# Order of the modulation and first products, and 32-column levels of the RWKV inverse, in a two-layer diffusion block

## The chip, the core and the metric

The kernel runs on one NeuronCore of a Trainium2 chip. The engines are TensorE (PE, its weight loads are listed as PEld), VectorE (DVE), ScalarE (ACT), GpSimd (POOL) and SyncE (SP, which only issues transfers here). The metric is the device time of one execution in microseconds (us), as the median of several runs. All arrays are 32-bit floats; PE multiplies either in full fp32 or, for the large weight products, as three fp32r products of high and low parts.

## What is computed

A hybrid block of two layers over 256 context and 256 latent tokens of width 1024. The parts that matter here:

```
mod_l = jnp.split((jax.nn.silu(c) @ ada_w[l] + ada_b[l])[:, None, :], 6, axis=-1)
mod_c = jnp.split(jax.nn.silu(c_ctx) @ ada_w[l] + ada_b[l], 6, axis=-1)
hl = modulate(rmsnorm(xl, norm_mix_pre[l]), mod_l[0], mod_l[1])     # h * (1 + scale) + shift
hc = modulate(rmsnorm(xc, norm_mix_pre[l]), mod_c[0], mod_c[1])
zl = hl @ w_in[l]
zc = hc @ w_in[l]
...
def step(s, inp):                       # branch D, RWKV-7, both directions
    r_t, w_t, k_t, v_t, kk_t, a_t = inp
    sa = jnp.einsum('bhvk,bhk->bhv', s, kk_t)
    s = (s * w_t[:, :, None, :] - sa[..., None] * (kk_t * a_t)[:, :, None, :]
         + v_t[..., None] * k_t[:, :, None, :])
    return s, (jnp.einsum('bhvk,bhk->bhv', s, r_t) if emit else None)
```

The kernel runs the recurrence in chunks of 64 tokens. Each chunk needs the inverse of a unit lower triangular 64x64 matrix, one for each of 4 heads and 8 chunks.

## The kernel before

**The first stage.** Everything is stored with features on the 128 partitions and the 512 tokens along the free axis, so the normalised input has 8 row tiles (k = 0 to 7) of 128x512. The shift and scale of row tiles 2q and 2q+1 come from two 256-column blocks of `ada_w`, blocks q and 4+q: this is modulation pair q. A pair is made on PE by two `mod` jobs (L1921, 8 products each) and two `modt` jobs (L1929, 2 products each) that fold four partial rows and turn them to columns. Between them ACT copies the row out of PSUM (`mrow`, L912), and after them DVE adds the bias (L1337) and forms the gain (`amod`, L1413). ACT then applies shift and scale to two row tiles (L953), rounds them to fp32r (`HR` high, L959), DVE makes the low part (L1401), ACT and DVE split two new tiles of `w_in` into `whi` (L899) and `wlo` (L1326). PE multiplies: `steps(ns, ks)` takes the output tiles ns over the row tiles ks, with three instructions for each pair (L1950, L1951, L1952). There are 6 output tiles in this stage (FIRST), so 6 x 8 x 3 = 144 products. Each engine works its list in order; ACT and DVE have the order pair q, its two row tiles, its two weight tiles, pair q+1. SP issues the loads in one queue: `ada` has 4 slots, so the blocks of pair 2 wait for the `mod` jobs of pair 0, those of pair 3 for the `mod` jobs of pair 1; behind them stand the constants and the next weight tiles. A weight slot of `ring` is free when its two `wlo` are made.

After the stage the remaining output tiles of z follow in `project` (L1878 to L1880), then attention, RWKV, gates, output projection and FFN, for two layers.

**The inverse.** For each layer and direction (4 passes) the inverse TN of all blocks starts at block size 2 and doubles over LEVELS = (2, 4, 8, 16, 32). A level z is, for each head pair p of two:

- `sx` (PE, L2120): LM1, stationary, times TN, moving, in 16 small products of 64x64, four of them side by side in the array
- a mask into XS (DVE, L1652) that keeps the block under the diagonal at this level
- `tt` (PE, L2108): four transposes of TN, copied to TT by ACT (L1153)
- one or several other jobs that are laid between (LM2 products L2082, `tok` transposes, `ta`, `xv`, `wl`/`al`, `kss`)
- `sy` (PE, L2159): TT, stationary, times XS, moving, again 16 products of 64x64
- TN = TN - sy (DVE, L1669)

PE takes sx p0, sx p1, tt p0, tt p1, the other jobs, sy p0, sy p1. DVE takes the two masks, other work, the two subtractions. sx of the next level waits for the subtraction of its p. After the last level two more transposes, and from them u0 and at, lead to the chain over the 8 chunks. XS has 64 columns for each block; only the columns whose block of size z is an even one (t // z even) can be other than zero after the mask.

Of the kernel before, what the change touches and what calls it, by code (L numbers as in the profile page):

```python
# [17 lines left out]
ALU = mybir.AluOpType  # L18
# [3 lines left out]
P = 128  # L22
# [4 lines left out]
LAT = 256  # L27
# [8 lines left out]
CH = 64  # L36
NCH = T // CH
NB = T // P
# [31 lines left out]
for _n, _c in VEC_COLS:  # L70
# [4 lines left out]

CONST_COLS = [("ones", P), ("fold", 2), ("ident", P), ("heads", P), ("swap", P), ("lm", 2 * CH), ("m1", CH),
              ("m2", CH), ("m4", CH), ("m8", CH), ("m16", CH), ("m32", CH), ("eye", CH), ("cos", LAT), ("sin", LAT),
# [21 lines left out]
def constants():  # L99
# [3 lines left out]
    def put(name, a):  # L103
        c[:, CON[name]:CON[name] + a.shape[1]] = a
# [13 lines left out]
    for z in LEVELS:  # L118
        put(f"m{z}", ((s // z) % 2 == 1) & (t // z == s // z - 1))
# [229 lines left out]
def build(nc, a, out):  # L349
    ctx = ExitStack()  # L350
    with ctx:
# [108 lines left out]
        XS = at("XS", 88, [2, 2, NB, CH])  # L460
# [124 lines left out]
        def bank(name):  # L585
            k = PLACE[name]
            return ps[:, k:k + 2, :] if name[0] in PAIRED else ps[:, k, :]

# [274 lines left out]
        def _(act):  # L863
# [96 lines left out]

            for q in range(4):
                fill(("start", 0, q))
                first_rows(2 * q)
                first_rows(2 * q + 1)
                first_high(2 * q)
                first_high(2 * q + 1)
                if q < 3:
                    split_until(2 * q + 2)
            for l in range(LAYERS):
# [339 lines left out]
        def _(dve):  # L1309
# [110 lines left out]
            for l in range(LAYERS):  # L1420
# [200 lines left out]
                for d in range(2):  # L1621
# [12 lines left out]

                    def square_mask(name):
                        return K(name, CH).unsqueeze(1).unsqueeze(1).to_broadcast([P, 2, NB, CH])
# [12 lines left out]
                    for n, z in enumerate(LEVELS):  # L1649
                        for p in range(2):  # L1650
                            s = blocks(filled(dve, ("sx", l, d, z, p)))
                            dve.tensor_tensor(XS[:, p, :, :, :], s, square_mask(f"m{z}"), ALU.mult)\  # L1652
                               .then_inc(frees(("sx", l, d, z, p)), 1)
# [8 lines left out]
                        for p in range(2):  # L1662
                            s = blocks(filled(dve, ("sy", l, d, z, p)))
                            t = TN[:, p, :, :, :].rearrange("p b y n -> p y b n")
                            if n:
                                emptied(dve, ("sy", l, d, LEVELS[n - 1], p))
                            else:
                                dve.wait_ge(t_done, 2 * it + p + 1)
                            dve.tensor_tensor(t, t, s, ALU.subtract).then_inc(frees(("sy", l, d, z, p)), 1)  # L1669
# [161 lines left out]
        def _(pe):  # L1831
# [101 lines left out]
            def first_products():  # L1933
# [22 lines left out]
                fill(("start", 0, 0))  # L1956
                steps(range(2), range(2))
                fill(("start", 0, 1))
                steps(range(2), range(2, 4))
                steps(range(2, 4), range(4))  # L1960
                fill(("start", 0, 2))
                steps(range(4), range(4, 6))
                steps(range(4, 6), range(6))
                fill(("start", 0, 3))
                steps(range(FIRST), range(6, KT))

            pe.wait_ge(silu_c, 1)
            for l in range(LAYERS):
# [96 lines left out]
                for d in range(2):  # L2065
# [45 lines left out]
                    for n, z in enumerate(LEVELS):  # L2111
                        for p in range(2):
# [6 lines left out]
                            for b, x, y in corners():  # L2119
                                last = pe.matmul(o[side(y), x, CH * b:CH * b + CH], LM1[side(x), 2 * p + y, b, 0:CH],  # L2120
                                                 TN[side(x), p, b, y, :], start=True, stop=True)
# [32 lines left out]
                        for p in range(2):  # L2154
# [3 lines left out]
                            for b, x, y in corners():  # L2158
                                last = pe.matmul(o[side(x), y, CH * b:CH * b + CH], TT[side(y), p, b, x, :],  # L2159
                                                 XS[side(y), p, x, b, :], start=True, stop=True)  # L2160
# [177 lines left out]
```

## Time and profile before

| | |
|---|---|
| runs, median (lowest to highest) | 1743.99 us (1742.7 to 1755.26), 3 runs |
| the profiled execution's own time | 1740.77 us, span 1739.0 us |
| mean granted TensorE clock | 0.973 |
| busy share of the span | PE 93%, PEld 76%, DVE 53%, ACT 45%, POOL 17% |

The span runs from the first to the last instruction. The profile page divides it into 40 slices, follows the chain that ended last, and groups instructions by line. Since PE is busy nearly everywhere, the stretches to look at are those in which it is not: the first 100 us, and the four passes of the inverse at about 350, 420, 1285 and 1348 us.

### The profile page before, as it was taken

The page shows a single profiled execution, that of the slowest core. Times are in us where ns is not written, and L with a number is a line of the kernel's source. Part 1 is how long each engine was busy: PE and PEld are TensorE (multiplying, and loading weights), DVE is VectorE, ACT ScalarE, POOL GpSimd, SP SyncE. Part 2 cuts the span into 40 slices and gives each one's busy share as a digit, 9 for nine tenths or more (in the row PEclk, how much of TensorE's full clock was granted, in tenths as well). Part 3 has the DMA queues.
Part 4 walks back from the last instruction along what each step waited for, and adds up shares of the span by engine and source line. Part 5 has one row for each costly group of instructions (what it writes and reads, how often), then busy time and mean ns, then how long its engine had stood idle before and what let it go on. Part 6 is the DMA issues. An engine that isn't in the chain of part 4 may idle for free.

```text
span 1739.0 us, 33048 instructions
## 1 busy us (share of the span) xinstructions
PE 1611.8 (93%) x14136; PEld 1321.1 (76%) x14136; DVE 913.3 (53%) x1438; ACT 783.1 (45%) x1285; POOL 302.3 (17%) x241
## 2 busy tenths in 40 slices
PE   5899999988899998899999998999988889989997
PEld 3678767776666676688888885887776679879997
DVE  3154445476334444555555224565786446567754
ACT  4232355473342233544444223624766453566653
POOL 0041033513010000011112000121452110012201
PEclk8899999999899999999999999999999999989999
DMA  9473345504682222132222534734523284436553
GB/s 324 107 190 98 112 159 176 176 7 148 185 301 73 96 73 73 49 97 97 97 97 62 124 100 148 222 124 134 168 66 124 55 278 155 145 98 194 182 164 116
DMA packets 230496, 234.49 MB, mean 135 GB/s; under 512 B 5904, under 2 KB 217232, under 8 KB 230224
## 3 DMA queue, kind: packets, MB, share of 16 engines
q1 hardware_dynamic: 210720, 190.17, 34.6%
q0 software_dynamic: 15024, 35.92, 7.6%
q10 hardware_dynamic: 4608, 6.29, 1.1%
q8 instruction: 113, 1.85, 0.5%
q14 instruction: 31, 0.25, 0.0%
HBM read 216.63 MB, written 15.73 MB: 134 GB/s over the span
## 4 chain that ended last, share of the span: by engine, by line
PE 67%; DVE 5%; issue 3%; ACT 3%; DMA 0%; POOL 0%; ACTq 0%; DVEq 0%; POOLq 0%
PE ps L1878 16%; PE ps L1879 16%; PE ps L1880 16%; PE ps L2262 5%; PE ps L2120 2%; PE ps L2108 1%; PE ps L1921 1%; PE ps L2159 1%; DVE X L1392 1%; PE ps L2082 1%; PE ps L1901 1%; DVE wlo L1326 1%; PE ps L1902 1%; PE ps L1903 1%; PE ps L1859 1%
## 5 line engine op out<-in xcount | busy, mean ns | idle before, releaser
L899 ACT ACTIVATE whi<-ring 128x1024 fp32r<-128x1024 f32 (+1 forms) x264 | 275.3, 1046 | 550.7 <-PE ps L1880 493.1
L1326 DVE TENSOR_TENSOR wlo<-ring,whi 128x1024 fp32r<-128x1024 f32 (+1 forms) x264 | 326.5, 1242 | 218.5 <-ACT whi L899 217.8
L1878 PE MATMUL ps<-H,whi 128*128 128x512 f32 (+1 forms) x656 | 220.6, 336 | 2.2 <-DVE wlo L1326 2.2
L1880 PE MATMUL ps<-H,wlo 128*128 128x512 f32 (+1 forms) x656 | 220.4, 336 | 0.0
L1879 PE MATMUL ps<-H,whi 128*128 128x512 f32 (+1 forms) x656 | 220.4, 336 | 0.0
L1878 PE MATMUL ps<-HR,whi 128*128 128x512 f32 (+1 forms) x568 | 202.2, 356 | 2.2 <-DVE wlo L1326 1.8
L1880 PE MATMUL ps<-HR,wlo 128*128 128x512 f32 (+1 forms) x568 | 198.3, 349 | 0.0
L1879 PE MATMUL ps<-HR,whi 128*128 128x512 f32 (+1 forms) x568 | 198.1, 349 | 0.0
L1878 PEld LDWEIGHTS ps<-H,whi 128*128 128x128 f32 x656 | 124.5, 190 | 15.6 <-issue 2.8
L1880 PEld LDWEIGHTS ps<-H,wlo 128*128 128x128 f32 x656 | 124.5, 190 | 12.9
L1879 PEld LDWEIGHTS ps<-H,whi 128*128 128x128 f32 x656 | 124.5, 190 | 12.5
L1878 PEld LDWEIGHTS ps<-HR,whi 128*128 128x128 f32 x568 | 107.5, 189 | 20.0 <-issue 5.4
L1879 PEld LDWEIGHTS ps<-HR,whi 128*128 128x128 f32 x568 | 107.6, 189 | 14.0 <-issue 0.7
L1880 PEld LDWEIGHTS ps<-HR,wlo 128*128 128x128 f32 x568 | 107.5, 189 | 14.1
L799 POOL TENSOR_SCALAR pr<-pr,stat 128x512 f32<-128x512 f32 (+1 forms) x48 | 71.3, 1498 | 246.4 <-DVE stat L1597 246.4
L1878 PE MATMUL ps<-UA,whi 128*128 128x512 f32 (+1 forms) x320 | 107.6, 336 | 0.0
L1879 PE MATMUL ps<-UA,whi 128*128 128x512 f32 (+1 forms) x320 | 107.5, 336 | 0.0
L1880 PE MATMUL ps<-UA,wlo 128*128 128x512 f32 (+1 forms) x320 | 107.5, 336 | 0.0
L855 POOL TENSOR_TENSOR CU<-CU,rs 128x512 f32<-128x512 f32 (+1 forms) x22 | 39.5, 1796 | 373.3 <-ACT rs L1294 373.3
L1878 PE MATMUL ps<-HG,whi 128*128 128x512 f32 (+1 forms) x256 | 91.7, 358 | 0.0
L2262 PE MATMUL ps<-YB,WB 128*128 128x512 f32 (+1 forms) x256 | 87.0, 492 | 4.2 <-DVE YB L1755 4.2
L1879 PE MATMUL ps<-HG,whi 128*128 128x512 f32 (+1 forms) x256 | 86.7, 339 | 0.0
(318 smaller groups left out, 3064.2 us busy)
## 6 DMA issues: line engine op xcount, KB each, us to landing
ring<-in_ffn_up SPq DMA_DIRECT2D x44, 1024.0 KB, 5.1
ring<-in_ada_w SPq DMA_DIRECT2D x40, 1024.0 KB, 5.6
ring<-in_w_gate SPq DMA_DIRECT2D x32, 1024.0 KB, 6.1
ring<-in_w_in SPq DMA_DIRECT2D x24, 1024.0 KB, 7.2
ring<-in_ffn_down SPq DMA_DIRECT2D x32, 512.0 KB, 4.0
ada<-in_ada_w SPq DMA_DIRECT2D x8, 1024.0 KB, 11.9
WB<-in_w_branch POOLq DMA_DIRECT2D x8, 1024.0 KB, 7.5
ring<-in_w_o SPq DMA_DIRECT2D x8, 1024.0 KB, 5.2
```

What stands on the lines that cost most here:

```text
L799: pool.tensor_scalar(pr[:, u % 4, 0:nk], pr[:, u % 4, 0:nk], stat[:, 2, u % 4:u % 4 + 1], None, ALU.mult).then_inc(p_ready, 1)
L855: pool.tensor_tensor(u, u, (rs, rt)[j % 2][:, c0:c1], ALU.mult).then_inc(u_ready, 1)
L899: act.activation(whi[half_slot(m)][:, 0:kn, :], ring[:, SLOT[raw] % RING, 0:kn, P * half:P * half + P], ACT.Copy).then_inc(hi_done, 1)
L1326: dve.tensor_tensor(wlo[half_slot(m)][:, 0:kn, :], ring[:, SLOT[raw] % RING, 0:kn, P * half:P * half + P], whi[half_slot(m)][:, 0:kn, :].b ...
L1392: ins = dve.scalar_tensor_tensor(x, O[:, i - 1, 256 * s:256 * s + 256], amod[:, k, i - 1, s:s + 1], x, ALU.mult, ALU.add)
L1859: last = pe.matmul(o[:, c0:c1], K("ones"), src[:, i, c0:c1], start=(i == 0), stop=(i == KT - 1))
L1878: pe.matmul(o[:, c0:c1], hi[:, i, :], part(0, k), start=(k == 0), stop=False)
L1879: pe.matmul(o[:, c0:c1], hi[:, i, :], part(1, k), start=False, stop=False)
L1880: last = pe.matmul(o[:, c0:c1], lo[:, i, :], part(0, k), start=False, stop=(k == kn - 1))
L1901: pe.matmul(o, hi[:, k, :], part(0, k)[:, c0:c1], start=(k == 0), stop=False)
L2120: last = pe.matmul(o[side(y), x, CH * b:CH * b + CH], LM1[side(x), 2 * p + y, b, 0:CH], TN[side(x), p, b, y, :], start=True, stop=True)
L2262: last = pe.matmul(o[:, c0:c1], wb[:, 2 * i + k, P * (j % 2):P * (j % 2) + P], YB[:, 2 * i + k, c0:c1], start=(k == 0), stop=(k == 1))
```

## The change

Two things are changed.

In the first stage, PE makes modulation pair 1 before any product, and pair q+1 before the products with the row tiles of pair q. `steps` is cut accordingly. ACT's code is written in another order, too, but its instructions come out in the same order as before, and so do those of DVE and SP.

In the inverse, sx multiplies only the even blocks of TN's columns (a strided moving operand), so it streams 32 columns and not 64; its mask constants, XS and the sy product have 32 columns for each block; and the subtraction touches only the even blocks of TN (again strided). The helper `even_blocks` picks these columns.

```
+CH2 = CH // 2
     for z in LEVELS:
-        put(f"m{z}", ((s // z) % 2 == 1) & (t // z == s // z - 1))
+        even = t[:, (t[0] // z) % 2 == 0]
+        put(f"m{z}", ((s // z) % 2 == 1) & (even // z == s // z - 1))
...
+        def even_blocks(v, z):
+
+            if len(v.shape) == 2:
+                return v.rearrange("p (g two n) -> p g two n", two=2, n=z)[:, :, 0, :]
+            return v.rearrange("p b y (g two n) -> p b y g two n", two=2, n=z)[:, :, :, :, 0, :]
...
-                            s = blocks(filled(dve, ("sx", l, d, z, p)))
-                            dve.tensor_tensor(XS[:, p, :, :, :], s, square_mask(f"m{z}"), ALU.mult)\
+                            s = filled(dve, ("sx", l, d, z, p))[:, :, 0:NB * CH2].rearrange("p x (b n) -> p x b n", b=NB)
+                            dve.tensor_tensor(XS[:, p, :, :, :], s, half_mask(f"m{z}"), ALU.mult)\
...
-                            s = blocks(filled(dve, ("sy", l, d, z, p)))
-                            t = TN[:, p, :, :, :].rearrange("p b y n -> p y b n")
+                            s = filled(dve, ("sy", l, d, z, p))[:, :, 0:NB * CH2]                                .rearrange("p y (b g n) -> p b y g n", b=NB, n=z)
+                            t = even_blocks(TN[:, p, :, :, :], z)
...
                 fill(("start", 0, 0))
+                fill(("start", 0, 1))
                 steps(range(2), range(2))
-                fill(("start", 0, 1))
-                steps(range(2), range(2, 4))
-                steps(range(2, 4), range(4))
+                steps(range(2, 4), range(2))
                 fill(("start", 0, 2))
-                steps(range(4), range(4, 6))
-                steps(range(4, 6), range(6))
+                steps(range(4), range(2, 4))
+                steps(range(4, 6), range(4))
                 fill(("start", 0, 3))
+                steps(range(FIRST), range(4, 6))
                 steps(range(FIRST), range(6, KT))
...
-                                last = pe.matmul(o[side(y), x, CH * b:CH * b + CH], LM1[side(x), 2 * p + y, b, 0:CH],
-                                                 TN[side(x), p, b, y, :], start=True, stop=True)
+                                last = pe.matmul(o[side(y), x, CH2 * b:CH2 * b + CH2].rearrange("k (g n) -> k g n", n=z),
+                                                 LM1[side(x), 2 * p + y, b, 0:CH], even_blocks(TN[side(x), p, b, y, :], z),
+                                                 start=True, stop=True)
```

On PE, at the start of the first stage, the list before is (`whi_70` to `whi_75` are the high parts of output tiles 0 to 5, `wlo_76` to `wlo_81` the low ones; line numbers of the changed kernel are 12 higher here):

```order
L1921 MATMUL ps<-ada,cpad 32x256 x16
L1929 MATMUL ps<-con,mrow 128x2 x4
L1950 MATMUL ps<-HR,whi_70 128x512
L1951 MATMUL ps<-HR,whi_70 128x512
L1952 MATMUL ps<-HR,wlo_76 128x512
...
L1950 MATMUL ps<-HR,whi_71 128x512
...
L1921 MATMUL ps<-ada,cpad 32x256 x16
L1929 MATMUL ps<-con,mrow 128x2 x4
L1950 MATMUL ps<-HR,whi_70 128x512
```

and of the change:

```order
L1933 MATMUL ps<-ada,cpad 32x256 x16
L1941 MATMUL ps<-con,mrow 128x2 x4
L1933 MATMUL ps<-ada,cpad 32x256 x16
L1941 MATMUL ps<-con,mrow 128x2 x4
L1962 MATMUL ps<-HR,whi_70 128x512
...
L1962 MATMUL ps<-HR,whi_71 128x512
...
L1962 MATMUL ps<-HR,whi_72 128x512
...
L1962 MATMUL ps<-HR,whi_73 128x512
...
L1933 MATMUL ps<-ada,cpad 32x256 x16
L1941 MATMUL ps<-con,mrow 128x2 x4
```

The second pair (L1921 before, L1933 after) has moved in front of the first product, and the products of output tiles 2 and 3 with the first two row tiles have moved in front of the third pair. The blocks of products between the pairs are 12, 36, 60 and 36 before, and 0, 24, 48 and 72 after.

In the first level of a pass (z = 2), PE's rows before, where the sx and sy jobs of both p stand as L2120 and L2159, with the transposes and the LM2 products around them:

```order
L2120 MATMUL ps<-TN,LM_90 64x64 x32
L2108 MATMUL ps<-con,TN 128x128 x8
...
L2159 MATMUL ps<-XS,TT 64x64 x32
L2120 MATMUL ps<-TN,LM_90 64x64 x32
L2108 MATMUL ps<-con,TN 128x128 x8
```

and after:

```order
L2132 MATMUL ps<-TN,LM_90 64x32 x32
L2120 MATMUL ps<-con,TN 128x128 x8
...
L2172 MATMUL ps<-XS,TT 64x32 x32
L2132 MATMUL ps<-TN,LM_90 64x32 x32
L2120 MATMUL ps<-con,TN 128x128 x8
```

Nothing moved there: the products are as many, with a 64-column stationary operand as before, and half the moving columns. On DVE the masks become `XS<-ps,con 128x256` (from 128x512), and the subtractions `TN<-TN,ps 128x128x2` at z = 2 down to `128x8x32` at z = 32 (from 128x2x4x64): 256 elements, in runs of z.

## Rows read from the trace of the kernel before

**Rows 1.** The page: its span, and part 1, busy us, share, instructions.
```profile
span 1739.0 us, 33048 instructions
...
PE 1611.8 (93%) x14136; PEld 1321.1 (76%) x14136; DVE 913.3 (53%) x1438; ACT 783.1 (45%) x1285; POOL 302.3 (17%) x241
```
**Rows 2.** Waits from 0 to 95 us: total us, times, longest.
```profile
PE ps L1950 <- DVE HR L1401: 11.6, 3, 3.9
...
PE ps L1950 <- DVE wlo L1326: 9.1, 1, 9.1
```
**Rows 3.** Timeline from 33.6 us: start, us, engine, line, operation, [idle before].
```profile
33.67 1.93 PE L1921 MATMUL ps<-ada,cpad 128*32 128x256 f32 x32
...
35.54 1.24 PE L1929 MATMUL ps<-con,mrow 128*128 128x2 f32 x8
...
37.28 2.07 ACT L953 ACTIVATE Z<-Z,mod,amod 128x256 f32<-128x256 f32 x4 [1.23 <-DVE amod L1413]
...
40.30 1.99 ACT L899 ACTIVATE whi<-ring 128x1024 fp32r<-128x1024 f32 x2
40.66 0.79 PE L1950 MATMUL ps<-HR,whi 128*128 128x512 f32 x1 [3.88 <-DVE HR L1401]
...
41.38 2.36 DVE L1326 TENSOR_TENSOR wlo<-ring,whi 128x1024 fp32r<-128x1024 f32 x2 [0.17 <-ACT whi L899]
```
**Rows 4.** Timeline around the first product.
```profile
26.98 1.98 ACT L899 ACTIVATE whi<-ring 128x1024 fp32r<-128x1024 f32 x2
...
29.33 0.80 PE L1950 MATMUL ps<-HR,whi 128*128 128x512 f32 x1 [9.14 <-DVE wlo L1326]
```
**Rows 5.** Timeline: the last product of the stage.
```profile
92.06 0.39 PE L1952 MATMUL ps<-HR,wlo 128*128 128x512 f32 x1
```
**Rows 6.** Stretches of PE: us, busy (instructions), granted clock, DMA share, GB/s.
```profile
22.40:28.90 6.50, 0.00 (x0) 0.50 1.10 348
...
32.40:39.10 6.70, 4.32 (x46) 1.00 1.10 348
39.20:45.90 6.70, 5.24 (x12) 0.50 1.07 375
...
87.00:93.00 6.00, 6.00 (x26) 1.00 0.78 42
```
**Rows 7.** DMA issues from 11.1 to 17.5 us (pair 1): KB each, us to landing.
```profile
ada<-in_ada_w SPq DMA_DIRECT2D x2, 1024.0 KB, 12.2
```
**Rows 8.** Timeline of level z = 4, first pass; L1669 of z = 2 stands first.
```profile
358.56 1.28 DVE L1669 TENSOR_TENSOR TN<-TN,ps 128x512 f32<-128x512 f32 x2
...
359.34 1.29 PE L2120 MATMUL ps<-TN,LM 64*64 64x64 f32 x64 [1.72 <-issue]
...
360.56 1.09 PE L2108 MATMUL ps<-con,TN 128*128 128x128 f32 x8
...
361.59 1.10 PE L2082 MATMUL ps<-ar,zk 64*64 64x128 f32 x32
...
363.68 1.16 PE L2159 MATMUL ps<-XS,TT 64*64 64x64 f32 x64
...
364.56 1.28 DVE L1669 TENSOR_TENSOR TN<-TN,ps 128x512 f32<-128x512 f32 x2
```
**Rows 9.** Timeline of the end of the first pass.
```profile
384.76 1.28 DVE L1669 TENSOR_TENSOR TN<-TN,ps 128x512 f32<-128x512 f32 x2 [2.31 <-PE ps L2159]
...
386.80 0.63 PE L2108 MATMUL ps<-con,TN 128*128 128x128 f32 x4 [0.64 <-DVE t L1504]
```
**Rows 10.** DVE groups by form: busy us, mean ns, idle before.
```profile
L1669 DVE TENSOR_TENSOR TN<-TN,ps 128x512 f32<-128x512 f32 x40 | 25.9, 684 | 41.0 <-PE ps L2159 41.0
...
L1588 DVE TENSOR_TENSOR E<-ps,bm 128x256 f32<-128x256 f32 x16 | 6.6, 415 | 0.0
...
L1732 DVE TENSOR_TENSOR YB<-YB,ps 64x512 f32<-64x512 f32 x4 | 2.7, 686 | 0.1
```
**Rows 11.** Timeline of PE, one `modt` job (two moving columns).
```profile
18.95 0.61 PE L1929 MATMUL ps<-con,mrow 128*128 128x2 f32 x4
```

More of the change, by code:

```diff
@@ L73 @@
 NVEC = _at
+CH2 = CH // 2
 CONST_COLS = [("ones", P), ("fold", 2), ("ident", P), ("heads", P), ("swap", P), ("lm", 2 * CH), ("m1", CH),
-              ("m2", CH), ("m4", CH), ("m8", CH), ("m16", CH), ("m32", CH), ("eye", CH), ("cos", LAT), ("sin", LAT),
+              ("m2", CH2), ("m4", CH2), ("m8", CH2), ("m16", CH2), ("m32", CH2), ("eye", CH), ("cos", LAT), ("sin", LAT),
               ("reset", T), ("window", GRID_W)]
@@ L459, in build @@
         TN = at("TN", 84, [2, NB, 2, CH])
-        XS = at("XS", 88, [2, 2, NB, CH])
+        XS = at("XS", 88, [2, 2, NB, CH2])
         XV = at("XV", 92, [2, 2, NB, CH])
@@ L959, in first_high @@
                 act.activation(HR[:, 0, i, :], Z[:, i, :], ACT.Copy).then_inc(h_hi, 1)
+            fill(("start", 0, 0))
             for q in range(4):
-                fill(("start", 0, q))
                 first_rows(2 * q)
@@ L968, in _ @@
                     split_until(2 * q + 2)
+                    fill(("start", 0, q + 1))
             for l in range(LAYERS):
@@ L1633, in masked, with half_mask @@
                                           ALU.mult).then_inc(frees((name, l, d, p)), 1)
+                    def half_mask(name):
+                        return K(name, CH2).unsqueeze(1).unsqueeze(1).to_broadcast([P, 2, NB, CH2])
                     def square_mask(name):
@@ L2158, in _ @@
                             for b, x, y in corners():
-                                last = pe.matmul(o[side(x), y, CH * b:CH * b + CH], TT[side(y), p, b, x, :],
+                                last = pe.matmul(o[side(x), y, CH2 * b:CH2 * b + CH2], TT[side(y), p, b, x, :],
                                                  XS[side(y), p, x, b, :], start=True, stop=True)
```

## The prediction

> **What bounds the kernel now.** I read the page first: the span is 1739.0 us and PE is busy for 93% of it [rows 1]. So time can only be won where PE waits, or where its own work shrinks. I then read the waits of the first 95 us. The products of the first stage waited 9.1 us for the first low weight half, and three times for the low part of a row tile, 11.6 us in all [rows 2]. The timeline of one such round says why. Pair 1 takes PE from 33.67 until 36.78 (35.54 + 1.24). Only then can ACT begin the row tiles (37.28), and the first product that needs them starts at 40.66, after 3.88 us with nothing to do on PE, since the pair stands directly in front of the products that need it [rows 3]. The stretches show a second price: after the idle time the granted clock is at its lower level, 1.2 GHz (0.50), and 12 products take 5.24 us, against 26 instructions in 6.00 us at 2.4 GHz, that is 0.43 us and 0.23 us for one [rows 6]. Last I read the passes of the inverse: DVE subtracts, PE multiplies, and in level z = 4 the two take turns [rows 8].
>
> **First stage, the step that is moved.** I follow PE in the new order with the old durations. From a round I take: pair to its end on PE 3.1 us, plus 0.33 in front; from its end, ACT's rows at +0.5, the first row tile's low part, and so the first product, at +3.9, the first low weight tile at 41.38 + 1.22, that is +5.8, the second 1.1 later [rows 3].
>
> Pair 1's weights are issued from 11.2 us on, the second at about 14.1, and land 12.2 us later, at 26.3 [rows 7]. PE has nothing else then, the two `mod` jobs end by about 28.3 even at the lower clock, which is granted from 22.4 on [rows 6]. But ACT copies their rows only behind the first two weight halves, which it finishes at 28.96 [rows 4]. The copies end near 29.7, and the two `modt` jobs behind them take 0.61 each at full clock [rows 11] and up to twice that at half. I put their end at 31.6, where the first product started at 29.33 before [rows 4]: a loss of 2.3 us. Then:
>
> - 12 products of tiles 0 and 1 at 0.425 (the clock is low): until 36.7
> - tiles 2 and 3 wait for their low halves, 31.6 + 5.8 = 37.4 and 38.5: 12 products at 0.23 end at 40.2. All this work was behind pair 1 before
> - pair 2, 3.45: until 43.65. SP issued the blocks of pair 2 as before
> - 24 products (rows 2 and 3, tiles 0 to 3), ready long since: until 49.1; the low halves of tiles 4 and 5 are there at 49.5 and 50.6; 24 products: until 55.0
> - pair 3, 3.45: until 58.4. Its weights can only come earlier than before, since SP waits for the `mod` jobs of pair 1, which now end 7 us sooner
> - 72 products without a wait, for the last row tiles are ready at 62.3 and wanted 36 products in, at 66.6: until 74.7
>
> Before, the last product starts at 92.06, so PE is free at 92.3 [rows 5]. The stage gains **17.6 us**. By kind: 11.6 us of waits [rows 2], 3.4 for pair 1, which now lies in PE's idle time, and about 6 for some 30 products fewer at the lower clock (0.2 each), less 2.3 at the start and 1.1 in new short waits. Bounds: if `modt` and the first 12 products find the clock high, 2 us more; if each of the two later pairs drops the clock again, a stretch of 6.7 at half speed [rows 6] costs 3.4, twice 6.8 us less. Through a pair with products before and after it the clock stayed high (4.32 of 6.7 us busy [rows 6]), so I take no drop. Behind the stage PE is busy without a wait until the attention, so what is won stays won; the halves of the next weights need the slots that tile 0 frees 6 products into the last block, 5 us before PE wants them.
>
> **Levels, the work that is made smaller.** DVE: both operations go from 512 to 256 elements; 684 ns at 512, and 415 ns for a product with a PSUM operand at 256 [rows 10], so 0.27 less. The runs are short and strided; the nearest row is a reversed operand (L1732, 686 ns for 512, every element a jump [rows 10]), and it costs nothing extra. I take 0.27 for all 80. The masks' half of it is worth nothing: PE is at the transposes and the LM2 products then and does not wait for XS [rows 8]. The subtractions lie on the path. Their two starts are 0.59 apart, the second ends at 358.56 + 1.28, and the second sx job starts then, 1.38 after the first subtraction starts. Now the first ends after 0.42, its sx starts at +0.52 and holds PE for 32 starts of 15 ns ((1.29 - 0.6) / 2 for each job's stream and a drain), that is until +1.0, while the second subtraction is over at +0.75. So the second sx starts 0.38 earlier, and all behind it: transposes, LM2, its mask, sy [rows 8]. This holds in 4 levels of each of the 4 passes: 16 x 0.38 = 6.1. In the first level nothing changes, because its sx waits for the start value of TN. At a pass's end, the second transposes wait for DVE's L1504 in the passes of direction 0, which stands behind both subtractions (384.76 until 386.80 [rows 9]): 0.27 x 2 = 0.53; in direction 1 PE is free after 0.55 and 0.31 is won. 2 x 0.53 + 2 x 0.31 = 1.7. Together **7.8 us**.
>
> PE: I take no gain from 32 columns. With a stationary operand of 128 columns an instruction with 2 moving columns starts every 0.12 us ((0.61 - 0.25) / 3 [rows 11]) and one with 128 as often ((1.09 - 0.27) / 7 = 0.12 [rows 8]): the weight load sets the pace. With 64 columns and four in parallel that would be 0.12 / 2 / 4 = 15 ns, and that is what sx has already (1.16 us for 64, less 0.22 for the last: 15 ns [rows 8]). The stationary operand keeps its 64 columns. Against it stands that LM2's products, 128 moving columns, start every 27 ns ((1.10 - 0.27) / 31 [rows 8]): from 128 to 64 the pace did halve. If it halves again, each pass wins 0.24 in its first level, 0.42 behind each of the four others' second sx, and 0.24 at three sy jobs, 2.6; four times, 10.6 us. The Trainium skill (TensorEngine Tiling, section Instruction Overhead) has a rule on the same question: a product with one moving column takes as long as one with 60. By it the 32 columns would cost as 60 and give nothing; by the halving the sum would be 10.6 larger. The trace has no 32-column product, so neither is shown here.
>
> **Sum.** 17.6 + 7.8 = 25.4. The profiled execution took 1740.8 us, 3.2 below the median of 1743.99; both should keep that distance. Profiled 1715.4, median **1718**.
>
> **Rivals.**
> 1. PE also runs at half the pace number: 1718 - 10.6 = 1707. For it the step from 27 to 15 ns, against it rows 11. Chance 0.12.
> 2. The first stage gives only part: the clock falls after each later pair, or ACT's copies come later: 6.8 back, 1725. The pairs have little work for PE at their end [rows 3]. Chance 0.11.
> 3. The levels win nothing: DVE pays for runs of 2 and 4 what it saves, or another job between ends last: 1718 + 7.8 = 1726. Against it rows 10. Chance 0.08.
> 4. Slower: PE reads the moving columns of TN in short pieces at a lower rate. Place: sx, twice in each of 20 levels. It decides from 25.4 / 40 = 0.64 us more for a job whose stream is 0.48, a factor of 2.3. At a factor of 3 and with sx alone, 40 x 0.96 = 38 lost, 1756. No row has a moving operand with a stride. Chance 0.04. That the change does nothing is excluded by the order, in which PE's rows moved.
>
> **How the numbers follow.** The forecast has 0.65; its own range is 1713 to 1723. Rival 1 has 0.12, rival 2 0.11, rival 3 0.08, rival 4 0.04. From 1706 (rival 1) to 1731 (rivals 2 and 3 with part of each other) more than 8 in 10 are inside. 1% of this kernel is 17.4 us, about what a measurement can tell from no change: faster needs less than 1726.6. That holds for the forecast, rival 1, and most of rivals 2 and 3, less something for both at once: 0.79. Within 1%: 0.17. Slower: 0.04.
>
> **What would show it.** In the new profile the last product of the stage starts near 74.5, the waits of the first products for HR are gone, PE waits about 0.7 and 0.4 us for `wlo`, and the granted clock stays high from about 36 us on. L1681 and L1664 last about 415 ns, the second sx follows the first without a gap, and 64 products of L2132 and of L2172 still take some 1.1 us: if 0.6, rival 1 holds; if 2 or more, rival 4. The passes shrink by about 2 us each. The forecast is wrong if pair 1's weights land after 28 us, if PE's start moves later than 32, or if the passes keep their length with shorter subtractions.

## The result and the profile after

The changed kernel takes 1725.74 us (median of 4 runs, 1725.01 to 1727.85), and the kernel before, run again beside it, 1747.78 (4 runs). The ratio is **0.986, 95% interval 0.9825 to 0.9895**. A second comparison, with 23 runs of the kernel before, gave 1723.7 against 1749.4, ratio 0.9854 (0.9827 to 0.988). So the change wins 22 to 26 us, as forecast (25.4), but the time is not 1718: the three runs of before from which the sum started lay 5 to 7 us under that kernel's usual time (1750.8 over 71 later runs).

| | before | after |
|---|---|---|
| profiled execution, span, us | 1739.0 | 1724.0 |
| last product of the first stage starts | 92.06 [rows 5] | 74.47 |
| one subtraction on DVE | 684 ns [rows 10] | 419 ns |
| the four passes, first sx to u0, us | 34.4, 36.2, 35.0, 33.2 | 33.0, 34.5, 34.0, 37.9 |

The page's span and its busy row. The span is 15.0 us shorter than in [rows 1], not 25:

```profile
span 1724.0 us, 33048 instructions
...
PE 1614.7 (94%) x14136; PEld 1324.6 (77%) x14136; DVE 894.4 (52%) x1438; ACT 782.3 (45%) x1285; POOL 302.2 (18%) x241
```

PE's waits up to 78 us (us in all, times, longest). The three waits for HR of [rows 2], 11.6 us, are gone, and so is the 9.1 us in front of the first product. In its place stand two waits inside the making of pair 1, and two later and short ones for `wlo`, 2.0 us together. The 3.5 us are named after `mod` here; in the profile of `e1_stage`, below, the same wait is named after the landing of the `ada` block.

```profile
PE ps L1933 <- DVE mod L1346: 3.5, 1, 3.5
PE ps L1941 <- ACT mrow L920: 2.4, 1, 2.4
PE ps L1962 <- DVE wlo L1335: 2.0, 2, 1.7
```

The timeline of the same stage (start, us, engine, line, [idle before]). Pair 1 is made from 24.8 to 31.8 us, then come the products, the longer of the two waits for a low half at 37.68, pair 2, and at 74.86 the next work:

```profile
24.82 3.29 PE L1933 MATMUL ps<-ada,cpad 128*32 128x256 f32 x32 [3.54 <-DVE mod L1346]
...
29.97 0.62 ACT L920 ACTIVATE mrow<-ps 128x256 f32<-128x256 f32 x2
30.47 1.33 PE L1941 MATMUL ps<-con,mrow 128*128 128x2 f32 x8 [2.36 <-ACT mrow L920]
31.66 0.77 PE L1962 MATMUL ps<-HR,whi 128*128 128x512 f32 x1
...
37.68 0.50 PE L1962 MATMUL ps<-HR,whi 128*128 128x512 f32 x1 [1.72 <-DVE wlo L1335]
...
40.62 1.93 PE L1933 MATMUL ps<-ada,cpad 128*32 128x256 f32 x32
...
74.86 1.52 PE L1998 MATMUL ps<-YB,con 128*128 128x512 f32 x3
```

DVE's groups by form: the masks (L1664) and the subtractions (L1681), 40 of each, against 684 ns in [rows 10]:

```profile
L1664 DVE TENSOR_TENSOR XS<-ps,con 128x256 f32<-128x256 f32 x40 | 16.6, 422 | 13.3 <-PE ps L2132 13.2
L1681 DVE TENSOR_TENSOR TN<-TN,ps 128x256 f32<-128x256 f32 x40 | 16.3, 419 | 48.6 <-PE ps L2172 48.2
```

The subtractions of level z = 4, which before are the last line of [rows 8], and sx of the level behind them. The two subtractions take 0.75 us together (1.28 before), and PE starts all 64 sx products in one piece 0.52 after the first subtraction starts. The two jobs take 1.14; sx had 1.29 in [rows 8] because its second job waited for the second subtraction, and sy, which did not wait, had 1.16:

```profile
346.52 0.75 DVE L1681 TENSOR_TENSOR TN<-TN,ps 128x256 f32<-128x256 f32 x2
347.04 1.14 PE L2132 MATMUL ps<-TN,LM 64*64 64x32 f32 x64 [0.26 <-issue]
```

From the start of one level to the next, pass 1 took 6.38, 6.00, 6.91 and 6.07 us before and takes 6.09, 5.57, 6.10 and 5.90: 1.70 in four levels, where the forecast has 4 x 0.38 = 1.52 (the second profile of before has 6.54 for the 6.91, and 1.42 in all). So both halves work as described, and yet the span gives only 15.0 of 25.4. Two stretches stand out. Behind pass 1 PE works without a gap at the lower of its two levels (granted 0.51, so 1.2 GHz), and the second half of pass 4 does the same:

```profile
386.00:400.00 14.00, 14.00 (x252) 0.51 0.61 202
1354.30:1366.00 11.70, 9.73 (x235) 0.56 0.41 92
```

The same place before (17.6 us later) had the full clock, and PE had work for 10.63 of the 14 us:

```profile
403.60:417.60 14.00, 10.63 (x329) 1.00 0.78 250
```

And PE pauses in pass 4, with nothing that it waits for by the profile ("issue"). First the changed kernel, then before, where the two pauses in front of the same products were 0.60 and 0.64:

```profile
1354.37 0.57 PE L2164 MATMUL ps<-X,LM 64*64 64x64 f32 x23 [3.10 <-issue]
...
1360.34 1.07 PE L2132 MATMUL ps<-TN,LM 64*64 64x32 f32 x30 [1.90 <-issue]
```

```profile
1370.57 0.57 PE L2151 MATMUL ps<-X,LM 64*64 64x64 f32 x23 [0.60 <-issue]
...
1374.75 0.69 PE L2120 MATMUL ps<-TN,LM 64*64 64x64 f32 x30 [0.64 <-issue]
```

Two questions are left: is what these stretches cost part of the change (did the shorter levels bring it), or do the two profiles only differ by chance? And what are the pauses?

### The profile page after: what moved, and what is told of

Its sections match the earlier page's. It is cut to its first block, busy times and chain, and to the rows that moved or that the text cites. A ratio compares the mean times of both kernels' runs of the same rounds, so it can differ in the third digit from the quotient of the medians.

```text
span 1724.0 us, 33048 instructions
## 1 busy us (share of the span) xinstructions
PE 1614.7 (94%) x14136; PEld 1324.6 (77%) x14136; DVE 894.4 (52%) x1438; ACT 782.3 (45%) x1285; POOL 302.2 (18%) x241
## 4 chain that ended last, share of the span: by engine, by line
PE 69%; DVE 5%; issue 3%; ACT 3%; DMA 0%; POOL 0%; ACTq 0%; DVEq 0%; POOLq 0%
PE ps L1890 16%; PE ps L1891 16%; PE ps L1892 16%; PE ps L2275 5%; PE ps L2132 1%; PE ps L2120 1%; PE ps L1933 1%; PE ps L2172 1%; DVE X L1401 1%; PE ps L2094 1%; PE ps L1913 1%; DVE wlo L1335 1%; PE ps L1914 1%; PE ps L1915 1%; PE ps L2207 1%
## 6 DMA issues: line engine op xcount, KB each, us to landing
ada<-in_ada_w SPq DMA_DIRECT2D x8, 1024.0 KB, 11.6
```

## The experiments

Each was timed against the kernel before on the same chip; "changed" is the changed kernel. Ratios are to the kernel before. They are compared with each other as ratios, since the kernel before itself had medians of 1749 to 1755 in these series.

### The two halves, and both

`e1_stage` has the new order of the first stage alone (PE's `fill` and `steps`, ACT's loop), on the levels of before.

> The kernel before with the new order of the first stage alone; the levels as before. By the forecast the stage is worth 17.6 us and nothing behind it gives any of it back: the next stage starts near 77 us in the profile where it started at 94.7 before, the four passes keep their lengths, and the time is 17.6 us below that of the kernel before (ratio 0.990). If instead the changed kernel's gain came in part from the levels having hidden a loss behind the stage (the lower clock falling on other work, because all of it now lies 17.6 us earlier), the stage still ends near 75 us but the time is only some 10 us lower (0.994).

Measured 1730.72 us against 1749.4, **ratio 0.990** (0.9871 to 0.9928). In its profile the last product starts at 73.44, and the four passes take 35.1, 37.7, 33.3 and 33.1, 0.4 us more in all than before. The first reading, 17.6 us, is met (17.5 by the ratio, 13 to 23 by its interval); the other, 0.994, lies outside the interval. In its profile the clock behind pass 1, where the changed kernel had 0.51, is high:

```profile
386.00:400.00 14.00, 10.78 (x344) 1.00 0.76 244
```

`e2_levels` has the levels alone.

> The kernel before with the 32-column levels alone. By the forecast 7.8 us less (ratio 0.9955): the second sx job of a level follows the first without a gap in 4 levels of each of the 4 passes, 0.38 us each, and the ends of the passes 1.7 in all. The rival is what the profile after suggests: the levels do get shorter, but pauses of PE for which the profile names no releaser, and stretches at the lower clock behind the passes, take part of it back. Then 0 to 4 us less (0.998 to 1.000), and the sum of the pauses in the passes is larger than in the profile of before.

Measured 1743.1 us (12 runs) against the same 1749.4, **ratio 0.9958** (0.994 to 0.9976), 7.3 us (4.2 to 10.5 by the interval; 6.3 by the medians): the forecast's 7.8, and just outside the 0 to 4 that the profiles suggested. Nor were its pauses clearly longer: at the four products in front of which PE pauses in passes 2 and 4 (see The pauses) it stood for 8.0 us in all, in the two profiles of before for 6.8 and 9.3.

`e3_after` is the changed kernel again.

> The changed kernel once more, beside its two halves on the same chip. If the two parts are independent, its gain is the sum of theirs: by the forecast 17.6 + 7.8 = 25.4 us (ratio 0.9854), by the first profile 15 to 22 us (0.987 to 0.991). Its profile shows what repeats: if the pause of 3.10 us at 1351 us and the lower clock from 386 to 400 us belong to the kernel they stand here again at the same instructions; if they are chance, their places and lengths differ.

Measured 1723.7 against 1749.4, **ratio 0.9854**, 25.5 us. The halves add up: 17.5 + 7.3 = 24.8. The pause in pass 4 stood again in front of the same product, with another length (2.55), and the clock behind pass 1 was low again.

`e0_before` is the kernel before again.

> The kernel before once more, for a second profile. Its first profile is of an execution of 1740.8 us, the shortest of all its runs (median of 23 runs 1749.4), with 45.8 us of PE work at the lower clock behind the first 95 us; the kernels with shorter DVE operations show 65 to 90. If the lower clock belongs to the shorter levels, this profile has 40 to 50 again. If an execution of common length of the kernel before simply has more of it, it has 55 to 70, its span is 5 to 10 us longer than 1739.0, and the difference of the first two profiles (15 us) is too small for that reason.

Its span was 1743.6 us, with 56.0 us of PE work at the lower clock behind the first 95 us (the busy time inside the trace's stretches at the lower level). That is the second case, if narrowly: the span is 4.6 us longer than 1739.0 and not 5 to 10. Its pass 4 took 37.7 us, as long as the changed kernel's, with pauses of 2.52 and 1.65 in front of those two products and the lower clock in the same place:

```profile
1372.00:1388.00 16.00, 12.20 (x286) 0.68 0.30 69
```

So pass 4 says nothing against the change; the first profile of before was of an execution that was spared there. The clock in the result of each run says the same of the whole kernel. Over 71 runs of before the time goes with the mean granted clock (correlation -0.90): 19 runs at 0.970 or more have a median of 1744.5 us, 18 runs at 0.962 or less 1756.4, and with each us more at the lower level goes 0.30 us more time (the slope of a straight line through the 71). The first profile of before was of clock 0.973 and 1740.8 us, that of after of 0.972, so two equal clocks were compared, of which one is uncommon for its kernel (median over 23 runs of before 0.967) and the other is common (0.971 over the runs of `e3_after`). The levels alone leave it where it was (0.966 against 0.967), the new stage alone raises it (0.971). From 0.967 to 0.971 is 14 us less at the lower level, by that slope some 4 us. The trace of the stage itself gives more: of its 144 products 44 start at the lower level before and 7 after (46 and 10 in the second profiles). With the 0.20 us that each costs more by [rows 6], 37 fewer are 7.4 us, where the forecast put about 6 on some 30 fewer.

Whether the shorter levels bring more of the lower clock stays open. Behind the first 95 us, all eleven profiles with subtractions of 256 elements have 63 to 90 us of PE work at the lower level, the three without 44 to 56. But these three are of executions whose clock lay above the median of their kernels' runs (0.973, 0.970 and 0.977 against 0.967, 0.9675 and 0.971), and over all runs the levels leave the mean clock as it was.

### What of the levels' gain is whose

`e4_y32`: the kernel before with 32 columns in sy and in the subtraction only (`...` marks what is left out of a line).

```
-  pe.matmul(o[side(x), y, CH * b:CH * b + CH], TT[...], XS[side(y), p, x, b, :], ...)
+  pe.matmul(o[side(x), y, 32 * b:32 * b + 32], TT[...],
+            XS[side(y), p, x, b, :].rearrange("k (g two n) -> k g two n", two=2, n=z)[:, :, 0, :], ...)
-  t = TN[:, p, :, :, :].rearrange("p b y n -> p y b n")
+  t = TN[:, p, :, :, :].rearrange("p b y (g two n) -> p b y g two n", two=2, n=z)[:, :, :, :, 0, :]
```

> The kernel before with 32 columns in the sy products and in the subtraction only; sx, the masks and XS keep 64 columns (their odd blocks are zero and are skipped). By the forecast the whole gain of the levels lies in the subtraction, so this kernel gains what the levels alone gain, 7.8 us by the forecast (ratio 0.9955), and its sx job of 64 products still takes 1.3 us. If the masks or the shorter sx carry part of it, this kernel gains less than the levels alone, by 2 us or more.

Measured 1743.64 us (12 runs), **ratio 0.9975** (0.9954 to 0.9996), 4.4 us. The ratios of the two kernels are 2.9 us apart, their medians 0.5 (1743.64 and 1743.1), and the intervals overlap: the time does not say whether the masks or the shorter sx carry 2 us. The traces do. The first two levels of pass 2, which nothing disturbs, take 5.72 and 5.34 us before, 5.45 and 4.94 here and 5.42 and 4.91 with the levels alone. Of 0.30 and 0.43 us, all but 0.03 is there with 32 columns in sy and in the subtraction only.

`e10_pe64`: the changed kernel with PE back at 64 columns, DVE still at 256 elements (its views are adapted, not shown).

```
-  pe.matmul(o[side(y), x, CH2 * b:CH2 * b + CH2]..., LM1[...], even_blocks(TN[side(x), p, b, y, :], z), ...)
+  pe.matmul(o[side(y), x, CH * b:CH * b + CH], LM1[...], TN[side(x), p, b, y, :], ...)
-  ..., TT[side(y), p, b, x, :], XS[side(y), p, x, b, :], ...
+  ..., TT[side(y), p, b, x, :], XS[side(y), p, x, b, :].unsqueeze(1).to_broadcast([CH, 2, CH2]), ...
```

> The changed kernel, but PE streams 64 columns again in sx and sy: sx takes all of TN, sy takes each 32-column block of XS twice (the second copy is written beside the first and never read). DVE keeps 256 elements in masks and subtractions. By the forecast the 32 columns on PE are worth nothing, so the ratio is that of the changed kernel, 0.985 to 0.986. A rival from the profiles of the first runs: the three kernels with 32 columns in sx or sy, and the changed one, show 70 to 81 us of PE work at the lower clock behind the first 95 us, the two with 64 columns 44 and 46, with new stretches at 386 to 400 us and 1356 to 1368 us. If the 32 columns bring the lower clock, these stretches are gone here and the kernel is some 12 us faster than the changed one (0.978). If the 32 columns do shorten PE's jobs, this kernel is 2 to 5 us slower than the changed one (0.987 to 0.988).

Measured 1725.61 against 1751.01, **ratio 0.9856** (0.9825 to 0.9888): the changed kernel's. The interval excludes the 10.6 us of rival 1 (0.9915), but not the 2 to 5 us of the expectation; the trace does. The same two levels of pass 2 take 5.45 and 4.94 us, 0.03 more than in the changed kernel: 32 columns on PE are worth some 0.6 us in all 20 levels. The rival on the clock falls, too: its profile has 90 us of work at the lower clock behind the first 95, more than any other. The same two jobs, at 64 columns:

```profile
346.46 0.77 DVE L1684 TENSOR_TENSOR TN<-TN,ps 128x256 f32<-128x256 f32 x2
346.98 1.16 PE L2135 MATMUL ps<-TN,LM 64*64 64x64 f32 x64 [0.23 <-issue]
```

1.16 us for 64 columns and 1.14 for 32, both starting 0.52 behind the subtraction: the moving columns do not set the pace of 15 ns. That the load of the stationary operand, 64 columns in both, does, as the prediction has it, fits; no run here changes its width. The Trainium skill (TensorEngine Tiling, section Instruction Overhead) says that a product with one moving column takes as long as one with 60. By that rule 32 columns save next to nothing against 64; the trace agrees, with 0.02 us in 64 products.

`e6_subtract_twice`: one more DVE operation of 256 elements ahead of each subtraction.

```
+  dve.tensor_tensor(XS[:, p, :, :, :], XS[:, p, :, :, :], half_mask(f"m{z}"), ALU.mult)
   dve.tensor_tensor(t, t, s, ALU.subtract).then_inc(frees(("sy", l, d, z, p)), 1)
```

> The changed kernel with one more DVE operation of 256 elements (some 0.4 us, a product of XS with a mask that nobody reads) ahead of each of the 40 subtractions. By the forecast the second sx job starts two operations behind the first subtraction's start, so 1.0 becomes 1.68: 0.68 in each of 16 levels, 10.9 us, and at the ends of the passes 2 x 0.84 and 2 x 0.6, together 13.8 us slower than the changed kernel (ratio 0.993), 6 us more than the gain of the levels. If the subtractions lie on the path only half of the time, some 7 us (0.9895).

Measured 1732.34 against 1751.01, **ratio 0.9902** (0.9868 to 0.9936): 8 us slower than the changed kernel, not 13.8. Its timeline of DVE gives the error in my number:

```profile
347.32 0.43 DVE L1681 TENSOR_TENSOR XS<-XS,con 128x256 f32<-128x256 f32 x1
347.67 0.41 DVE L1682 TENSOR_TENSOR TN<-TN,ps 128x256 f32<-128x256 f32 x1
348.00 0.42 DVE L1681 TENSOR_TENSOR XS<-XS,con 128x256 f32<-128x256 f32 x1
348.33 0.41 DVE L1682 TENSOR_TENSOR TN<-TN,ps 128x256 f32<-128x256 f32 x1
```

An operation takes 0.42, but one behind the other starts after 0.33 to 0.35. So the fourth ends 1.42 behind the first's start and the second sx starts at 1.52, 0.52 later than at 1.0, not 0.68. 16 x 0.52 = 8.3, and up to 2 at the ends of the passes, against 8 measured. The time alone would fit the other reading as well, that the subtractions lie on the path only half of the time (0.9895). The levels decide: those that nothing disturbs are 0.54 us longer each (5.45 against 4.91 in pass 2, 6.63 against 6.09 in pass 3), as the full price by the spacing asks. The subtractions lie on the path.

`e5_masks_twice`: each mask done twice, the first copy to a tile that nobody reads.

```
+  dve.tensor_tensor(XD[:, p, :, :, :], s, half_mask(f"m{z}"), ALU.mult)
   dve.tensor_tensor(XS[:, p, :, :, :], s, half_mask(f"m{z}"), ALU.mult)...
```

> The changed kernel with each of the 40 masks done twice (the first copy to a tile that nobody reads), one more DVE operation of 256 elements, spaced some 0.34 us behind the other, ahead of each. By the forecast the masks are not on the path, since PE is at the transposes and the LM2 products then: no change against the changed kernel (ratio 0.985 to 0.986). If they are on it, each of 20 levels gets 0.67 us longer, 13 us (0.993).

Measured 1722.2 against 1754.61, **ratio 0.9831** (0.9777 to 0.9885). The interval excludes 0.993, though not some 5 us; the levels do. The first two of pass 2 take 5.42 and 4.92 us, against 5.43 and 4.91 in the changed kernel. The masks have room and are not on the path.

### What of the stage's gain is whose

`e7_pair1`: the changed kernel with only pair 1 moved.

```
 fill(("start", 0, 0))
 fill(("start", 0, 1))
 steps(range(2), range(2))
 steps(range(2), range(2, 4))
 steps(range(2, 4), range(4))
 fill(("start", 0, 2))
...
```

> The changed kernel with only modulation pair 1 moved in front of the first product; pairs 2 and 3 stand directly in front of the products that need them, as before (blocks of 0, 48, 60 and 36 products between the pairs). By the forecast's method: first product at 31.6, 48 products until 44.9, pair 2 until 48.3, 3.9 us of waiting for its rows, 60 products with some of them at the lower clock until 68, pair 3 until 71.5, again 3.9 of waiting, 36 products until 86.5. So the stage wins some 6 of its 17.6 us, and the kernel is 11.6 slower than the changed one (ratio 0.992). If nearly all of the stage's gain comes from pair 1, which fills PE's idle time ahead of the first product, the stage ends before 80 us and the ratio is below 0.989.

Measured 1735.56 against 1751.01, **ratio 0.9917** (0.9889 to 0.9946), as worked out (0.992); the last product starts at 84.08, 2.4 us ahead of the estimate. Pairs 2 and 3 wait as before, each for its rows, 7.8 us in all:

```profile
50.99 0.80 PE L1962 MATMUL ps<-HR,whi 128*128 128x512 f32 x1 [3.88 <-DVE HR L1410]
PE ps L1962 <- DVE HR L1410: 7.8, 2, 3.9
```

So by the last product's start pair 1 brings 8 us of the stage's gain (92.06 to 84.08), and the work laid between pairs 2 and 3 and their products the other 10.

`e8_order`: PE's list as changed, ACT's (first piece) and DVE's (second piece) reordered.

```
-    split_until(2 * q + 2)
-    fill(("start", 0, q + 1))
+    fill(("start", 0, q + 1))
+    split_until((4, 6, 6)[q])
...
+    split_until((0, 4, 6, 6)[q])
     first_low(2 * q)
     first_low(2 * q + 1)
-    if q < 3:
-        split_until(2 * q + 2)
+    if q == 0:
+        split_until(2)
```

> The changed kernel with ACT and DVE reordered in the first stage: ACT copies the rows of pair 1 ahead of the first weight halves, and splits the halves of output tiles 2 and 3 ahead of the row tiles 2 and 3 (those of tiles 4 and 5 ahead of row tiles 4 and 5). PE's order is unchanged. By the forecast the stage now loses 2.3 us at its start because the copies stand behind two splits, and 1.7 us in the wait for the low half of tile 2. Without them the first product starts at 30.4 instead of 31.7, the wait of 1.72 at 37.7 is gone, and the stage ends at 72 instead of 74.9: 2.5 to 3 us faster than the changed kernel (ratio 0.984). If a later row tile or the landing of the third weight tile then ends last, a new wait of 1 to 3 us stands in front of the products of tiles 4 and 5, and nothing is won.

Measured 1723.97 against 1751.01, **ratio 0.9851** (0.9823 to 0.9879). In the profile it does what it should: the first product at 30.42, the last at 72.08 (74.47 in the first profile of the changed kernel, 73.56 in the second), and a wait of 0.7 left:

```profile
PE ps L1963 <- DVE wlo L1335: 0.7, 1, 0.7
```

The 1.5 to 2.4 us are too few for this measurement; in the time they are not shown.

### The pauses

In all twelve profiles taken with the HG load whole and at its old place, PE stands still in front of the same products, counted from a pass's first sx: number 630 of pass 2 (1.6 to 4.4 us), 625 and 750 of pass 4 (0.6 to 3.1 us), and in eleven of them 880 of pass 2 (0.95 to 4.5 us). The numbers lie 250 and 125 apart in their pass, and that is a first hint: the page lists 113 packets of 16 KB in a queue that carries instructions, one for every 125 of PE's 14136 products.

```profile
q8 instruction: 113, 1.85, 0.5%
```

POOL issues two loads into HG in each of these passes, of 2 MB in pass 2 and of 1 MB in pass 4 (the expectation below names 1 MB for each). `e9_load_late` issues these loads behind the pass.

```
   pool.wait_ge(h_saved[l], 32)
+  pool.wait_ge(mm_done, done_at(("at", l, 1, 1)))
   for part in range(2):
       pool.dma_start(HG[:, part, :, c0:T], hsave[part, ...])
```

> The changed kernel, but POOL issues the two 1 MB loads HG<-hsave of a layer only when PE has finished the at jobs behind the second pass, and no longer inside the pass. In all ten profiles so far PE pauses at the same two instructions of pass 2 (numbers 630 and 880 of its some 897 MATMULs) for 1.7 to 4.4 and 0.95 to 3.8 us, and of pass 4 (625 and 750) for 0.6 to 3.1 and 0.6 to 2.5 us, with no releaser. If an instruction load there waits behind the HG load, these pauses shrink to 0.5 us or less and passes 2 and 4 are 3 to 5 us shorter each, 6 to 10 us in all (ratio 0.980 to 0.982), unless the pauses only move to the chain of chunks behind the pass. If the pauses have nothing to do with the HG load, they stay, and the ratio is 0.985 to 0.986.

Measured 1726.55 against 1754.61, **ratio 0.9863** (0.9823 to 0.9903): nothing won. But the pauses in front of these products are gone (those left in the two passes, in other places, are of 0.3 to 0.9 us), pass 2 takes 28.2 us and pass 4 29.0, against 34.5 and 37.9. The DMA view says what stood in front of PE. From 421.5 to 425.5 us, just ahead of the pause that ends at 428.73, the changed kernel has 370 packets of HG and none of the queue that carries instructions; the same stretch without the HG load has one, of 16 KB (queue, kind: packets, MB, share of 16 engines). First the changed kernel, then `e9_load_late`:

```profile
q0 software_dynamic: 370, 0.76, 74.7%
```

```profile
q8 instruction: 1, 0.02, 1.8%
```

By the packet times, that block of instructions started to move at 422.69 with the queues empty, 0.9 us after product 505 (125 before 630) had started. In the changed kernel product 505 started at 422.06, the first packet of HG moved at 422.25, and the block only at 426.13; it took 1.0 us, and PE went on with product 630 at 428.73, 1.6 us after that. Smaller pauses of this kind need no load of HG: passes 1 and 3 have none, and PE stands for 0.4 to 1.0 us in front of product 784 of pass 1 in eight of the 14 profiles, and in front of 789 of pass 3 in four. Where the gain went is in the same profile. The load now meets the next weights, whose blocks land 11.4 us behind their issue and not 5.3 as in the changed kernel (medians of 3). PE waits for them, and then works for 20.5 us at the lower clock, which costs half of 18.4 us:

```profile
452.32 1.94 PE L1934 MATMUL ps<-ring,cpad 128*32 128x256 f32 x16 [4.78 <-DMA ring<-in_ada_w]
```

```profile
450.70:471.20 20.50, 18.40 (x241) 0.50 1.05 354
```

`e12_pieces` keeps the load where it was, but cuts it in eight, on the lists of `e8_order`.

```
-  for part in range(2):
-      pool.dma_start(HG[:, part, :, c0:T], ...).then_inc(h_back[l], 16)
+  for n in range(8):
+      part, k = n // 4, 2 * (n % 4)
+      if n:
+          pool.wait_ge(h_back[l], 16 * n)
+      pool.dma_start(HG[:, part, k:k + 2, c0:T], ...).then_inc(h_back[l], 16)
 ...
-  pe.wait_ge(h_back[l], 32)
+  pe.wait_ge(h_back[l], 16 * 8)
```

> The kernel of the reordered ACT and DVE list (which ended the first stage at 72.1 us in its profile), and HG<-hsave in 8 loads one after the other, each issued when the one before has landed, at the place in POOL's list where the changed kernel issues its 2. With the whole load behind the pass, passes 2 and 4 shrank by 6 and 9 us, but PE then waited 4.8 us for the next weights and the time stayed the same. Here the load begins as early as in the changed kernel, and at any time at most an eighth of it stands in the queues. If PE's pauses come from an instruction load that stands behind the whole HG load, those at instructions 630 and 880 of pass 2 and 625 and 750 of pass 4 fall to 1 us or less each, passes 2 and 4 are 29 to 32 us long, the weights come as early as before, and the ratio is 0.978 to 0.982. If what is won there is given back once more (the lower clock or the weights behind the pass), the passes are shorter but the ratio is 0.984 to 0.986. If the pauses depend only on whether any such load is under way, they stay above 2 us.

Measured **1716.7 us** (1714.66 to 1723.53) against 1749.49, **ratio 0.982** (0.9787 to 0.9852). It is the fastest of all kernels here: 33 us below the kernel before and some 7 below the changed one (1723.7 against 1749.4), 5 by the ratio to `e8_order`, its own kernel with the load whole. The two intervals overlap, but five of its six runs are below the fastest run of every other kernel (1719.51). Pass 2 takes 30.6 us and pass 4 29.0, and both are at the full clock (stretch, us, PE busy, clock):

```profile
400.90:431.40 30.50, 25.24 (x897) 1.00 0.25 73
1325.00:1354.00 29.00, 25.47 (x896) 1.00 0.16 40
```

against the changed kernel's

```profile
406.20:440.70 34.50, 28.29 (x899) 0.90 0.44 125
1330.10:1368.00 37.90, 28.84 (x896) 0.86 0.26 59
```

What is left of the pauses is 0.58, 1.51 and 0.92 us in pass 2 (630, 755 and 880) and 0.67 in pass 4 (750). That is the first case, with the ratio at its upper end. In `e8_order` the two passes took 37.0 and 32.1 us, so they shrank by 9.5, where the time gives some 5. Part of the difference shows: PE waits 2.9 us for weights behind pass 2, and pass 3 took 36.0 us against 33.9, with 10.2 us of it at the lower clock against 3.4.

## Why the prediction was right, and where it was not

- **The stage, 17.6 us: right.** 17.58 in the first profiles (from 94.69 to 77.11 at the first product of the next stage), 19.8 in the second ones (95.96 to 76.20), and 17.5 by the ratio of `e1_stage`. That 17.58 meets the 17.6 so closely is luck: the pairs of profiles differ by 2 us, and the working has a slip of 0.3, since its 74.7 is where the last product starts and is set against 92.3, where it ends before. The start was put at 31.6 and came at 31.66, with the copies behind two weight halves, as worked out; the first wait for a low half was 1.72 instead of 0.7, since 12 products at the start had the clock rise under them and ended at 36.0 instead of 36.7. The clock stayed high through pairs 2 and 3, so rival 2 did not come. More products than the 30 left the lower clock (37), and the later waits were 2.0 and not 1.1: these two about cancel.
- **The levels, 7.8 us: right.** 7.3 by the ratio of `e2_levels`; 415 ns forecast and 419 measured; 0.38 forecast for a level and 0.29 to 0.45 in the four in which both profiles of each kernel agree (5.72 to 5.43, 5.34 to 4.91, 5.69 to 5.24, 6.38 to 6.09). The second sx starts 0.98 behind the first subtraction, where 1.0 was worked out and 1.38 stood before. Rival 3 falls with `e2_levels`, rival 4 with the 1.14 us of the two sx jobs.
- **No gain from 32 columns on PE: right**, but for 0.03 us a level, by `e10_pe64`. Rival 1 falls. The reason given, that the weight load sets the pace, fits and is not shown.
- **Masks worth nothing: right** (`e5_masks_twice`).
- **The sum: wrong step, "the profiled execution took 1740.8 us, 3.2 below the median of 1743.99; both should keep that distance".** The forecast's gain of 25.4 stands against 22.0 and 25.7 measured, but 1718 against 1725.74, outside my own range of 1713 to 1723 and inside the wide one. Nor was the distance kept: the profiled execution of the changed kernel took 1725.75, the median itself. The start of the sum was the mis-sized term: three runs gave 1743.99 where 71 later ones have a median of 1750.8, and the profile was of one of the best. 1749.4 - 25.4 would have been 1724.0. The page showed the mean clock, 0.973, but not that it is usually 0.967; of three runs one at 1755.26 was the only sign. A sum counted from a profile inherits the luck of that execution, and its difference to another profile (15.0 us) inherits it twice.
- **Pauses and clock in the passes: missing from the forecast.** The levels were costed as if a pass were only its levels. The pauses in front of four products are as large as the whole gain of the levels in a pass and vary from run to run; they are where the next gain was (`e12_pieces`).

## What to carry to other kernels

Put a small chain that other engines must finish (here modulation to row tiles) one block of matrix work ahead of its user, and count the wait, the work that falls into idle time and the clock apart: they were 11.6, 3.4 and about 7 us, less some 4 for the later start and new short waits. Where DVE and PE take turns, halve DVE's elements, which pays by its spacing, and expect next to nothing from going from 64 to 32 moving columns if the stationary operand stays as wide. And look for pauses without a releaser in front of the same instruction in several profiles: they may be instruction loads that stand behind a large transfer, which cutting the transfer in pieces mends.

## What the runs showed of the hardware

- PE's instructions come in blocks of 16 KB through DMA queue 8, one for 125 products here (113 blocks, 14136 products), and a block that is wanted while a load of 1 or 2 MB fills the queues can be late by 3 us (426.13 and 422.69). The pause in front of product 630 was 1.6 to 4.4 us with the load whole, 0.58 with it in eight pieces, and none with it elsewhere.
- DVE operations of 256 fp32 elements last 0.42 us but start every 0.33 to 0.35 us back to back. Runs of 2, 4 or 8 elements cost nothing extra: 417, 415 and 421 ns for a subtraction at these levels, 422 and 421 with runs of 16 and 32, 415 for a dense one in [rows 10].
- PE's small products with a 64-column stationary operand, four side by side, start every 15 ns with 32 moving columns as with 64 (two jobs of 32 take 1.14 and 1.16 us).
- The granted clock differs from run to run of the same kernel (means of 0.956 to 0.974 in 71 runs), and with it the time by 0.30 us for each us at the lower level. What decides whether the stretch behind pass 1 (386 to 400 us) is at the lower level stays open: it was so, for 3 to 14 us, in 9 of 11 profiles of kernels with 256-element subtractions and in none of the three without the change in the levels, yet over all runs the levels leave the mean clock as it was.
